# Hybrid encoder layer: gated attention passes interleaved, one store of the bias base, and the last down projection placed behind the expert loop

## The reference

```python
def gla_direction(q, k, v, log_a, strict):
    ...
    bcum = jnp.cumsum(log_a.astype(jnp.float32).reshape(B, H, n, CHUNK, dk), axis=-2)
    ...
    scores = jnp.einsum('bhnid,bhnjd,bhnijd->bhnij', qc, kc, decay)
    o_intra = jnp.einsum('bhnij,bhnjv->bhniv', scores, vc)
    u = jnp.einsum('bhncd,bhncv->bhndv', kc * jnp.exp(b_last - bcum), vc)
    ...
    o_inter = jnp.einsum('bhncd,bhndv->bhncv', qc * jnp.exp(bcum), s_in)
    return (o_intra + o_inter).reshape(B, H, S, dv)
```

## Time and profile before

| | us |
|---|---|
| median of 3 runs | 2732.44 |
| lowest, highest | 2729.37, 2736.33 |
| profiled execution | 2719.98 |
| its span | 2718.2 |
| PE busy | 2442.7 (90%) |
| DVE busy | 1840.1 (68%) |
| ACT busy | 1303.5 (48%) |
| POOL busy | 383.1 (14%) |
| loads of `w_up`, of `w_down` | 267, 128 |

### The profile page before, as it was taken

One profiled execution on the slowest core, in us unless ns is written; L12 is line 12 of the kernel. 1 busy time (PEld: TensorE's weight loads), 2 busy tenths in 40 slices (PEclk: granted clock), 3 DMA queues, 4 the chain that ended last, 5 costly groups with the idle time before them and its releaser, 6 DMA issues.

```text
span 2718.2 us, 38787 instructions
## 1 busy us (share of the span) xinstructions
PE 2442.7 (90%) x13622; PEld 1989.0 (73%) x13689; DVE 1840.1 (68%) x1900; ACT 1303.5 (48%) x1414; POOL 383.1 (14%) x321
## 2 busy tenths in 40 slices
PE   4999849689897995799999999999999999999994
PEld 3889646579764994677777787777777777777773
DVE  4399684821314226688887887778777788888776
ACT  4212353521223123466665665556555556766555
POOL 0000000001000043122221212112111111221211
PEclk9999966879899976899999999999999999999997
DMA  3111210211010046898987987779877799999776
GB/s 119 47 52 43 88 36 16 64 62 55 31 47 1 1 152 166 279 359 303 333 307 265 295 302 244 244 247 336 280 256 248 257 297 302 339 363 318 250 242 246
DMA packets 268700, 536.36 MB, mean 197 GB/s; under 512 B 11100, under 2 KB 45200, under 8 KB 268528
## 3 DMA queue, kind: packets, MB, share of 16 engines
q1 hardware_dynamic: 249952, 474.51, 49.6%
q0 software_dynamic: 16384, 57.68, 9.1%
q10 hardware_dynamic: 2288, 3.08, 0.4%
HBM read 491.45 MB, written 43.78 MB: 197 GB/s over the span
## 4 chain that ended last, share of the span: by engine, by line
PE 77%; DVE 12%; issue 4%; ACT 4%; DMA 2%; DVEq 1%; ACTq 0%; POOL 0%; POOLq 0%; SPq 0%
PE PS L2123 12%; PE PS L2125 11%; PE PS L2124 11%; PE PS L1782 9%; PE PS L2131 6%; PE PS L2128 6%; PE PS L1946 3%; PE PS L2012 3%; DVE wlo L1577 1%; PE PS L2093 1%; PE PS L1999 1%; PE PS L1964 1%; PE PS L1966 1%; PE PS L1965 1%; ACT whi L896 1%
## 5 line engine op out<-in xcount | busy, mean ns | idle before, releaser
L1577 DVE TENSOR_TENSOR wlo<-raw,whi 128x2048 fp32r<-128x2048 f32 x395 | 897.7, 2288 | 200.3 <-ACT whi L896 183.2
L896 ACT CAST whi<-raw 128x2048 fp32r<-128x2048 f32 x395 | 745.9, 1911 | 200.7 <-PE PS L2131 136.9
L2123 PE MATMUL PS<-whi,xhi 128*128 128x512 f32 x1056 | 438.5, 415 | 34.4 <-DVE yb L1660 18.5
L2125 PE MATMUL PS<-whi,xlo 128*128 128x512 f32 x1056 | 414.0, 392 | 0.0
L2124 PE MATMUL PS<-wlo,xhi 128*128 128x512 f32 x1056 | 412.3, 390 | 0.0
L2125 PEld LDWEIGHTS PS<-whi,xlo 128*128 128x128 f32 x1056 | 198.9, 188 | 43.7
L2124 PEld LDWEIGHTS PS<-wlo,xhi 128*128 128x128 f32 x1056 | 199.3, 189 | 40.2
L2123 PEld LDWEIGHTS PS<-whi,xhi 128*128 128x128 f32 x1056 | 200.5, 190 | 38.1 <-DVE wlo L1577 3.6
L2123 PE MATMUL PS<-whi,hhi 128*128 128x512 f32 x512 | 202.6, 396 | 0.0
L2125 PE MATMUL PS<-whi,hlo 128*128 128x512 f32 x512 | 199.7, 390 | 0.0
L2124 PE MATMUL PS<-wlo,hhi 128*128 128x512 f32 x512 | 199.4, 389 | 0.0
(11 more groups left out here) (380 smaller groups left out, 4626.2 us busy)
## 6 DMA issues: line engine op xcount, KB each, us to landing
raw<-in_exp_w_up SPq DMA_DIRECT2D x267, 1024.0 KB, 6.3
raw<-in_exp_w_down SPq DMA_DIRECT2D x128, 1024.0 KB, 7.3
ring<-in_w_in SPq DMA_DIRECT2D x11, 1024.0 KB, 5.3
xres<-in_x SPq DMA_DIRECT2D x4, 1024.0 KB, 12.7
ring<-in_xattn_wk SPq DMA_DIRECT2D x4, 1024.0 KB, 7.8
...
```

The source lines that it names most:

```text
L896: nc.scalar.copy(whi[:, chunk_slot(c, NSPL), :], raw[chunk_slot(c, NRAW)][:]).then_inc(s_whi, 1)
L1577: nc.vector.tensor_tensor(wlo[:, chunk_slot(c, NSPL), :], raw[chunk_slot(c, NRAW)][:], whi[:, chunk_slot(c, NSPL), :].bitcast(F), ALU.subtract
L2123: pe.matmul(o, hi[:, k, :], wh, start=first and bias is None, stop=False)
L2125: ins = pe.matmul(o, lo[:, k, :], wh, start=False, stop=stop and kk == 3)
```

## The change

**Gated attention.** The code of a pass is cut into functions, and the order of both passes is written out on each engine. Pass 0 takes all eight memory chunks. Pass 1's gates, minima, decays, keys to the window ends and queries from the window starts are made right behind pass 0's updates; pass 0's values are placed between the first score levels of pass 1, and pass 1's turned keys, updates and state steps between its levels 3 to 7, so that only its values stand behind its last level. For that pass 1 has tiles of its own (`Ssc1`, `ST1`, `KE1`, `KQf1`), which lie in the weight ring's space; so w_out's chunk `g_out` waits for the second turned keys and the next ones for the last value, with the reload of x behind them in SyncE's queue. In a value, the scores' products of both heads come first, then for each direction the two heads' state products, one from partitions 0 to 63 and one from 64 to 127.

**Bias base.** Each of the 16 bias products gets a second product into the same bank, the identity times `xres`, in fp32, so that a drained row holds residual and bias. SyncE stores these rows with 8 plain DMAs; the earlier stores of the residual and GpSimd's 8 accumulating DMAs are gone. Six bias products stand ahead of the token map, ten behind it. For the first gathers GpSimd leaves out a small multiply (L519).

**Expert loop.** `last_` is `used_` minus 1 and the loop is `Fori(1, NVIS)`, so 31 rounds are done and 21 skipped. The down projection of the last visit, with the load, cast and low part of its chunks (numbered 15 to 18), its drain and its scatter, stands behind the loop on each engine. The up projection and the turns of the visit behind the last are gone.

The core of the diff:

```diff
-        KEt = sb("KEt", [P, 4, 512], F, 48)
+        KEt = sb("KEt", [P, 4, 512], F, 173)
+        KQf1 = sb("KQf1", [P, 2, S], F, 0)
+        KE = [KQ2, sb("KE1", [P, 2, S], F, 24)]
...
-        Ssc = sb("Ssc", [P, 2, TT, P], F, 157)
+        Ssc = [sb("Ssc0", [P, 2, TT, P], F, 157), sb("Ssc1", [P, 2, TT, P], F, 16)]
...
-        ST = sb("ST", [P, 2, TT, P], F, 165)
+        ST = [sb("ST0", [P, 2, TT, P], F, 165), sb("ST1", [P, 2, TT, P], F, 8)]
...
+        def products_of(p, step):
+            base = {"ends": (8, 10), "starts": (9, 11)}
+            return base[step][p] if step in base else (0, 11)[p] + step + 1
+        def decayed_q(p):
+            return (kT[:, 0, :], qT[:, 0, :]) if p == 0 else (KQf1[:, 0, :], KQf1[:, 1, :])
+        def value_banks(p, w):
+            return 4 + 2 * (w % 2) if p == 0 else 2 * (w % 4)
+        STEPS_AFTER = {3: (0, 4), 4: (4, 8), 5: (8, 12), 6: (12, 14)}
...
+                if g == g_out:
+                    sp.wait_ge(s_ket, 8)
+                if g == g_out + 1:
+                    sp.wait_ge(s_op, 32)
...
-                sp.wait_ge(s_dr["o"], 3 * TT + t + 1)
-                sp.dma_start(acc_dram[P * t:P * (t + 1), :], xres[:, t, :]).then_inc(s_acc, 16)
-            for t in range(TT):
...
+                if last:
+                    j = c - 15
+                    w, e, col = w_dn, e_dn, 512 * (j // 2)
...
+            last_ = sp.value_load(usedb[0:1, 0:1], min_val=0, max_val=NVIS - 1)
             e0, e1 = expert(0), expert(1)
             for c in range(4, 8):
                 load_chunk(0, c, e0, None, fresh=True)
-            sp.wait_ge(s_bacc, 16 * TT)
+            for t in range(TT):
+                sp.wait_ge(s_bdr, 2 * (t + 1))
+                sp.dma_start(acc_dram[P * t:P * (t + 1), :], xres[:, t, :]).then_inc(s_acc, 16)
+            sp.wait_ge(s_acc, 16 * TT)
             for c in range(8, 4 + NRAW):
...
+            with sp.Fori(1, NVIS) as t:
+                with sp.If(t <= last_):
...
+            e_last = expert(last_)
+            for c in range(15, 19):
+                load_chunk(last_, c, None, e_last, last=True)
+            wait_multiplied(sp, last_, 14)
...
+                if not isinstance(t, int):
+                    nc.gpsimd.tensor_tensor(vt[:, 3, 1:2], pmod[:, 0:1], pmod[:, 1:2], ALU.mult)
...
-            pool.wait_ge(s_acc, 16 * TT)
-            for t in range(TT):
-                pool.wait_ge(s_bdr, 2 * (t + 1))
-                nc.gpsimd.indirect_dma_start(acc_dram, bass.IndirectOffsetOnAxis(
-                    ap=rowid[:, t:t + 1].bitcast(U32), axis=0), xres[:, t, :], None, compute_op=ALU.add
-                    ).then_inc(s_bacc, 16)
...
+            scatter(last_)
...
+            softplus(1)
+            window_decays(1)
+            exps(1, "ends")
+            exps_from_starts(1)
+            drain_values(0, range(4))
+            exps(1, 0)
+            exps(1, 1)
+            drain_values(0, (4, 5))
+            exps(1, 2)
+            place_halves(1)
+            drain_values(0, (6, 7))
+            exps(1, 3)
+            place_quarters(1)
+            keys_turned(1)
+            for l in range(4, 7):
+                exps(1, l)
+            place_diagonal(1)
+            act.wait_ge(s_lnv, 19)
+            act.wait_ge(s_plc, 6)
+            split_y(1)
+            split_w_out(0)
+            drain_values(1, range(TT))
...
+            for n in range(EARLY_BASE):
+                base_rows(n)
...
+            both_last = has_tail(last_)
+            split_hi(last_, 15)
+            for c in range(16, 19):
+                wait_lo(act, last_, c - NSPL)
+                split_hi(last_, c, first=True)
+            drain_rows(last_ + 1, 0, both_last, c0=1)
+            drain_rows(last_ + 1, 1, both_last, c0=1)
...
+            gate_minima(1)
+            empty_states(0)
+            states(0, 0, 14)
+            nc.vector.tensor_tensor(rg, rg, ngb[:].unsqueeze(1).broadcast_to([P, TT * GH, GDV]), ALU.mult
+                                    ).then_inc(s_rg, 1)
+            cumulated(1)
+            exponents_to_ends()
+            keys_to_ends(1)
+            queries_from_starts(1)
+            exponents(0)
+            empty_states(1)
+            for l in range(7):
+                if l >= 2:
+                    dve.wait_ge(s_gram, 2 * (8 + l))
+                if l == 1:
+                    dve.wait_ge(s_ket, 4)
+                to = (KQ, KQ2)[l % 2]
+                decayed(1, l, (to[:, 0, :], to[:, 1, :]), kT[:, 1, :], qT[:, 1, :])
+                if l < 6:
+                    exponents(l + 1)
+                if l in DIAG:
+                    select(1, l)
+                if l in STEPS_AFTER:
+                    states(1, *STEPS_AFTER[l])
+            select(1, 7)
...
+            step(nc.vector.tensor_scalar(usedb[:], vend[:, E - 1:E], 1.0, None, ALU.subtract))
...
+            def values(p, windows):
+                for w in windows:
+                    if w == 0:
+                        pe.wait_ge(s_kq, products_of(p, "starts"))
+                        pe.wait_ge(s_st, 14 * (p + 1))
+                        pe.wait_ge(s_plc, 3 * (p + 1))
+                    ahead = 2 if p == 0 else 4
+                    if w >= ahead:
+                        pe.wait_ge(s_oe, 16 * p + 2 * (w - ahead) + 2)
                     tw = slice(P * w, P * (w + 1))
-                    pe.matmul(o, Ssc[:, hh, w, :], v_tm[:, w, P * h:P * (h + 1)], start=True, stop=False)
-                    pe.matmul(o, KQ[hp, 0, tw], ST[hp, 0, w, :], start=False, stop=False)
-                    pe.matmul(o, KQ[hp, 1, tw], ST[hp, 1, w, :], start=False, stop=True).then_inc(s_op, 1)
+                    o = [PS[:, value_banks(p, w) + hh, 0:P] for hh in range(2)]
+                    for hh in range(2):
+                        h = 2 * p + hh
+                        pe.matmul(o[hh], Ssc[p][:, hh, w, :], v_tm[:, w, P * h:P * (h + 1)], start=True, stop=False)
+                    for d in range(2):
+                        for hh in range(2):
+                            hp = slice(GDK * hh, GDK * (hh + 1))
+                            ins = pe.matmul(o[hh], decayed_q(p)[d][hp, tw], ST[p][hp, d, w, :], start=False,
+                                            stop=d == 1)
+                            if d == 1:
+                                ins.then_inc(s_op, 1)
+            gates(0)
+            memory_chunk(0)
+            memory_chunk(1)
+            scores(0, 0)
+            memory_chunk(2)
+            memory_chunk(3)
+            for l in range(1, 8):
+                scores(0, l)
+                memory_chunk(4 + (l - 1) // 2, ((l - 1) % 2,))
+            memory_chunk(7, (1,))
+            turn_keys(0)
+            pe.wait_ge(s_sel, 6)
+            gates(1)
+            updates(0, 0, 14)
+            scores(1, 0)
+            values(0, range(4))
+            scores(1, 1)
+            values(0, (4, 5))
+            scores(1, 2)
+            values(0, (6, 7))
+            turn_keys(1)
+            scores(1, 3)
+            updates(1, 0, 4)
+            scores(1, 4)
+            updates(1, 4, 8)
+            scores(1, 5)
+            updates(1, 8, 12)
+            scores(1, 6)
+            updates(1, 12, 14)
+            scores(1, 7)
+            values(1, range(TT))
...
-                          start=True, stop=True).then_inc(s_bd, 1)
+                          start=True, stop=False)
+                pe.matmul(PS[:, i % 4, :], ident[:], xres[:, t, 512 * b:512 * (b + 1)], start=False, stop=True
+                          ).then_inc(s_bd, 1)
             pe.wait_ge(s_gde, 2)
             pe.wait_ge(s_bup, 9)
-            for i in range(2 * TT):
+            for i in range(EARLY_BASE):
...
+            for i in range(EARLY_BASE, 2 * TT):
+                down_bias(i)
...
+            def down(t, both, c0=8, read=2):
                 def all_groups(tail):
                     for i in range(2):
-                        pe.wait_ge(s_g if i == 0 else s_upr, 2 * t + 2)
+                        pe.wait_ge(s_g if i == 0 else s_upr, 2 * t + read)
                         for half in range(2):
-                            c = 8 + 2 * i + half
+                            c = c0 + 2 * i + half
...
+            down(last_ + 1, pe.snap(tail_last, min_val=0, max_val=1), c0=3, read=0)
```

409 lines of the change are left out of this document (208 added, 201 removed).

## The result

| | before | after |
|---|---|---|
| median, us | 2732.6 | 2672.26 |
| lowest, highest | 2729.37, 2736.33 | 2670.94, 2674.16 |
| profiled execution, span | 2719.98, 2718.2 | 2674.16, 2672.0 |
| PE busy, DVE busy | 2442.7, 1840.1 | 2400.5, 1815.1 |
| loads of `w_up` | 267 | 259 |

The ratio is 0.9779, with a 95% interval of 0.9762 to 0.9796: 60 us less, where I had forecast 41. The spans of the two profiles differ by 46.2 us only, because the profiled execution of before (2719.98) was shorter than every other one of it on record (2722.21 is the next); the last sections say where such differences come from.

What follows compares the result with a forecast made beforehand. The prediction read TensorE as 77% of the chain of waits and VectorE as 12%. Its terms, 28 + 6 + 7 = 41 us, taken from the median of 2732.44, gave 2691.4 us, with a range of 2676 to 2712.

Steps and rivals of the forecast that it cites:

- A: Gated attention: earlier start and faster pace of pass 1's values gain 28 us, from 15 to 39.
- B: Start of the experts: an earlier turn and first products at full clock gain 6 us, from -5 to +8.
- C: End of the kernel: one up projection with its turns goes, the loop's skipped rounds stand open; gain 7 us.
- pass 1's gates ... at half clock, 7.19: Gated attention: pass 1's gates run beside the key copies, take 7.19 us at half clock and end at 420.
- the window of 2.75 us: Values: a window of two heads takes 2.6 us with paired state products, 2.75 with joins, against 3.74 before.
- My sign of being wrong, a pace above 8: Gated attention: the forecast is wrong if pass 1's levels pace above 8 us; 6 to 8.5 was laid out.
- The rival of the higher clock: Values at the higher clock or more side by side: window 1.9 us, gain 38, time 2681; chance 0.13.
- not side by side: State products don't run side by side at 128 columns: window 3.74 us, gain 15, time 2704; chance 0.17.
- at 2.4 GHz: Start of the experts: the turn and first products run at full clock because TensorE was busy until then; 2.6 us more.
- I take its price as ScalarE's: Loop's end: a skipped round costs TensorE what it costs ScalarE, 0.43 us, 9.03 for 21 rounds.
- the rival with 1.58 us a round: Loop's end: TensorE's skipped rounds are dear, the end's gain becomes -13 and the time 2711; chance 0.08.
- the gain without anything between, 15: End: without anything between, the last down projection starts at 2646.3 instead of 2662.7, and the gain is 15 us.

Runs made afterwards that it cites:

- A alone: The kernel before with only the interleaved gated attention of the change: 2681.55 us, ratio 0.9831.
- the exact loop and the hint: The changed kernel with the loop ending at the number of rounds read from the table, plus a prefetch hint for TensorE's closing branch: 2657.14 us, ratio 0.9730.
- extra products: The changed kernel with 94 small unread TensorE products around pass 1's last levels: 2668.66 us; two more such kernels with the exact loop count: 2658.71 and 2657.86.
- B alone: The kernel before with only the bias base as a matmul, the plain stores and the split bias groups: 2720.38 us, ratio 0.9966.
- the exact loop: The changed kernel with the expert loop ending at the number of rounds read from the table, so no round is skipped: 2655.55 us, ratio 0.9732.

## Why the prediction was right or wrong

The direction was right, and so were the mechanisms, but the forecast of 2691.4 missed 2672.3 by 19 us. By parts: A 48 instead of 28, B 9 instead of 6, C 2.6 instead of 7. Two things make the miss. The sum was too small: from profiled to profiled execution the change is 45.8 us where I had 41, and in it A, read at the first output product, was 11.5 too small (39.5 for 28), while C's error went the other way and hid a part of that. And I put the sum on the median with an offset that did not hold, 14 us (last paragraph). The steps of the sum that failed are "pass 1's gates ... at half clock, 7.19" with the pace of the levels behind them, which led to 514.8, and the window of 2.75 us.

**A: the mechanism right, two terms too small.** What was predicted is there: pass 0's values inside pass 1's levels, the idle stretch behind window 1 of pass 0 (19.59 us), and values right behind the last scores.
- *The start of the values*, laid out to 514.8, was 508.2 in the first profile. About 4 us of the 6.6 come from "pass 1's gates ... at half clock, 7.19": I took the clock of the old order into the new one. In the new order TensorE had just had 32 records of memory products; the gates took 3.70 at a granted clock of 1.00 and ended at 415.4 instead of 420, and the turned keys took 1.94 for the 3.65 of the earlier trace rows. The lead stays nearly whole through the state steps (ended at 427.7 for my 431.5) to the queries from the starts (450.6 for 454.9) and is 3.1 at the first level product (459.2 for 462.3). The other 3.5 are the levels. From their first product to the values they took 49.0 us, and I had 52.5: VectorE started the first levels 5.5 to 5.9 us apart and the last three 9.6, 8.5 and 8.5. My sign of being wrong, a pace above 8, came true in those three, and the sum was still shorter than mine.
- *The window*, 2.75, was 2.31, below even the 2.6 that I had called the floor. Eight windows make 3.5 us. The floor was wrong because I paired the state products alone; the two heads' products of scores also start closer, 4 records in 1.15 us instead of twice 0.73, and no run shows why. The Trainium skill (TensorE: Matmul & The Clock Gate, Part 3 on packing small matmuls) says that matmuls on different row groups overlap. The trace agrees: 64-row products of 128 columns do (8 records of both heads in 1.23 us, 4 of one head in 1.22). The 2.6 that I had worked out from it is not what was measured.
- *Two small terms.* I took the drained end, 537.7, from the last product's end, 566.5, which is 0.9 too little; and I charged 1 for late w_out chunks, while the first output product came 19.1 us behind the values and 18.8 before. With these, 28 and 6.6 and 3.5 make 39.7, and the first profile shows 39.5.
- *The rival of the higher clock* had a chance of 0.13 and is half true. In the second profile of the changed kernel and in that of A alone the clock rises in the third window, and the values take 12.4 and 12.5 us instead of 18.5; with the exact loop and the hint it rises in the fifth, 15.0. In the other three profiles with alternated windows and no extra products it doesn't rise. What decides it was not found.
- By the marks of the profiles, that is by when a given product starts: seven profiles without A start the output projection at 586.4 in the mean, six with A (windows alternated, no extra products) at 544.3. That is 42.1 of the 48. From there to the first bias product the seven take 458.2 in the mean and the six 456.1, 2.1 more. The other 4 have no place in the marks and are within the interval of 40 to 52.
- The rival *not side by side* had A = 15 and 2704. The kernel with one head after the other took 2694: without the alternation A is worth about 22 (48.1 less 26.5).

**B: near in size, partly by luck, and something that no term held.** In the marks it is 5.5 us up to the first hidden rows: 4.8 up to the turn (I had 3.2) and 0.9 from there to the first product. Of the 2.6 us "at 2.4 GHz" only the turn's 0.9 came: after it TensorE idles 2.9 us for the token copies, and the products begin at the lower clock for 5.0 us. That is no shorter than without B, where it lasts 2.9 us in the profile of the earlier trace rows and 3.4 to 5.9 in the six others. So a turn that came earlier than forecast made up for a clock gain that did not come. That chunks 8 and 9 are wanted at 1098 and cost "nothing" overlooked that the first visit moves up too: the chain of the changed profile runs through chunk 8,

```profile
1040.92 3.89 DMA acc_scratch<-xres
...
1044.99 8.32 DMA raw<-in_exp_w_up
```

from the last store's landing to its load. The load was issued 42.9 us behind the first bias product and landed 51.3 behind it; before it was 35.0 and 43.2. ScalarE's cast of it now waits for the load (8.25 us, to 1053.34), where before it waited for TensorE, and TensorE stops for 1.40 us at 1054.41 (0.57 in the second profile, 0.35 with B alone, and not at all in the seven profiles without B). The cost is small: from the first product to the first hidden rows it is 33.9 us in the first profile and 32.7 in the second, against 31.9 to 33.2 without B. The marks leave 3.7 us of the 9.2 (whose interval is 6 to 13) without a place. The stop at the loop's first return is my candidate, 6 to 8 us in some executions without B; its share in the timed ones was not measured, so this stays open. The profiled execution of before had none of it, so no row showed it.

**C: the step that failed is "I take its price as ScalarE's".** My bound for VectorE, 0.62 us a skipped round, was the value (12.93/21 = 0.616), and I wrote "no more than 4 us later than ScalarE": it was 3.2 at the low part's start (2614.61, where ScalarE's cast ended at 2611.4). The down projection then started 22.8 us after the last turn instead of 19.0, and took 20.8 instead of the 20.0 I had allowed. Together that is 4.6 us later, and C fell from 7 to 2.6. TensorE's own skip is hidden under its wait of 21 us, so its price stays unknown, but the rival with 1.58 us a round (33 in all) didn't come. What I called the gain without anything between, 15, is near what the exact loop shows: 12.3 and 2.6, some 3 of it from the rounds that are done.

**The sum against the median.** I put the sum, made on one profiled execution, on the median of the others. The profiled one was 12.5 us under the median, and I took this offset as fixed. It wasn't: the changed kernel's profiled execution is 2 above its median. Of the 19 us missed, 14 are this offset: from profiled to profiled execution the change is 45.8 us, 5 more than my sum. In one session 26 executions of before spread over 15 us (2723.68 to 2738.86). That is a term that should have widened the range by several us on the fast side, since whatever made the others slower could go with the change. That it did go with the change is shown for none of the parts.
